# Attention units moved half a unit earlier, and three program blocks joined into one

## The reference

```python
h = rms_norm(x, norm_w[0])
proj = h @ w_in                                    # N_IN = 3668 columns
hm = mlstm_chunkwise(...)                          # 4 heads, running state
score = sum_h w[t,h] * relu(q_idx[t,h] . k_idx[s]) # DSA: indexer
_, sel = lax.top_k(score, 256)                     # each query keeps 256 keys
ha = softmax over the kept keys, times v           # 4 heads
hs = ssd_mixer(...)                                # Mamba-2, 8 heads, running state
x = x + rms_norm(concat([hm, ha, hs]) @ w_out, norm_w[1])
h = rms_norm(x, norm_w[2])
x = x + rms_norm((silu(h @ w_gate) * (h @ w_up)) @ w_down, norm_w[3])
```

## Time and profile before

| | us |
|---|---|
| median of 3 runs | 2692.28 |
| lowest and highest | 2689.32, 2702.49 |
| the profiled execution | 2698.94 |
| its span, first to last instruction | 2697.1 |
| TensorE busy | 2576.8 (96% of the span) |
| mean granted TensorE clock | 0.977 |

### The profile page before, as it was taken

How to read it: one execution, slowest core, us unless ns; L and a number is a source line. 1 busy time by engine, 2 the same in 40 slices (tenths; PEclk the granted TensorE clock), 3 DMA queues, 4 the chain that set the end, 5 groups by cost and what they waited for, 6 DMA issues and landing times. The chain is left out here.

```text
span 2697.1 us, 35783 instructions
## 1 busy us (share of the span) xinstructions
PE 2576.8 (96%) x12676; PEld 2074.7 (77%) x12676; DVE 1832.0 (68%) x3004; ACT 1092.5 (41%) x2078; POOL 1232.3 (46%) x778
## 2 busy tenths in 40 slices
PE   6999998999899999999989999988999999999997
PEld 5678876878688888888766787767877888888886
DVE  5679965773866666666665899648657666666666
ACT  4337435664422232232343463457554223232223
POOL 1348311422754455555433582114227455555545
PEclk8999999899999999999999999989999999999999
DMA  4213321532111111111431233124211111111113
GB/s 136 59 36 94 115 67 35 169 101 77 55 63 47 48 47 52 57 48 61 138 98 36 52 94 112 55 86 148 94 63 63 47 48 47 62 47 62 62 47 133
DMA packets 185793, 199.81 MB, mean 74 GB/s; under 512 B 17680, under 2 KB 161168, under 8 KB 185664
## 3 DMA queue, kind: packets, MB, share of 16 engines
q1 hardware_dynamic: 179904, 177.15, 21.3%
q10 hardware_dynamic: 5760, 20.97, 2.1%
HBM read 157.08 MB, written 38.80 MB: 73 GB/s over the span
## 5 line engine op out<-in xcount | busy, mean ns | idle before, releaser
L2295 POOL TENSOR_TENSOR ring_lo<-ring_sum,ring_hi 128x512 fp32r<-128x512 f32 x200 | 305.4, 1542 | 477.2 <-ACT ring_hi L2383 477.2
L2517 PE MATMUL ps<-form_hi,ring_hi 128*128 128x512 f32 x1232 | 484.5, 393 | 22.6 <-POOL ring_lo L1548 19.7
L2517 PE MATMUL ps<-form_lo,ring_hi 128*128 128x512 f32 x1232 | 482.5, 392 | 0.0
L2517 PE MATMUL ps<-form_hi,ring_lo 128*128 128x512 f32 x1232 | 482.4, 392 | 0.0
L931 PE MATMUL ps<-act_hi,whi 128*128 128x512 f32 x928 | 376.6, 406 | 8.5 <-ACT smr L430 8.4
L2605 DVE TENSOR_TENSOR yacc<-yacc,ps 128x1024 f32<-128x1024 f32 x176 | 214.7, 1220 | 243.7 <-PE ps L2543 243.7
L2383 ACT ACTIVATE ring_hi<-ring_sum 128x512 fp32r<-128x512 f32 x200 | 125.2, 632 | 629.4 <-DVE ring_sum L2593 629.2
L931 PE MATMUL ps<-act_hi,wlo 128*128 128x512 f32 x928 | 366.2, 395 | 0.0
L931 PE MATMUL ps<-act_lo,whi 128*128 128x512 f32 x928 | 365.5, 394 | 0.0
L1350 DVE TENSOR_SCALAR_CACHE_REDUCE ties<-score,kth 128x384 uint8<-128x384 f32 (+5 forms) x396 | 348.4, 942 | 6.1 <-issue 1.7
L636 POOL TENSOR_TENSOR wlo<-raw,whi 128x1024 fp32r<-128x1024 f32 x54 | 131.7, 2439 | 401.2 <-ACT whi L691 401.2
(11 more groups left out here) (333 smaller groups left out, 4606.4 us busy)
## 6 DMA issues: line engine op xcount, KB each, us to landing
raw<-in_w_in SPq DMA_DIRECT2D x56, 512.0 KB, 3.9
ff_raw<-in_w_gate SPq DMA_DIRECT2D x22, 1024.0 KB, 5.4
ff_raw<-in_w_up SPq DMA_DIRECT2D x22, 1024.0 KB, 5.3
ff_raw<-in_w_down SPq DMA_DIRECT2D x22, 1024.0 KB, 4.9
proj_scratch<-stage ACTq DMA_DIRECT2D x40, 512.0 KB, 2.7
wc<-proj_scratch SPq DMA_DIRECT2D x14, 1280.0 KB, 7.1
xmid_scratch<-xres SPq DMA_DIRECT2D x16, 512.0 KB, 2.6
resid<-xmid_scratch SPq DMA_DIRECT2D x16, 512.0 KB, 6.3
```

The lines of the kernel that those rows point to most:

```text
L2295: pool.tensor_tensor(flat_form(ring_lo[slot]), src, flat_form(ring_hi[slot]).bitcast(F32), ALU.subtract)\
L2517: mm = pe.matmul(ps[:, product_bank(r, i), :], w[:, k], a[:, k], start=(k == 0 and m == 0), stop=(k == 3 and m == 2))
```

## The change

1. `U_LATE` is 25 and `LEAD` is 4: call 8 of the attention stands behind eighth 4 of unit 25, and call 35 behind eighth 7 of unit 28. No call is left behind the projection.
2. From step 16 on, ScalarE does a pair's two exponentials together at the odd call, behind the copy of the turned weights.
3. ScalarE loads its table for logarithm and exponential ahead of unit 25, not at the start of stage B.
4. `kept_hi` of blocks 0 to 3 waits for the first half of unit 28 alone, those of 4 to 6 come at the end of stage A, and that of 7 behind the first four `rows` of stage B. The subtractions `kept_lo` of blocks 4 to 7 are all in GpSimd's stage B.
5. All stages are in one block. In place of the meeting, each engine waits for what it takes over: TensorE for the last copy out of PSUM, and further on for the attention's last steps and the cleared places; GpSimd for the last products with `v`; SyncE, ahead of chunk 1, for all eight `kept_lo` (`c_low`).

```diff
-U_LATE = 26
+U_LATE = 25
+LEAD = 4
@@ stage A, ScalarE and TensorE (the same order of calls)
                     if u >= U_LATE:
-                        k = EARLY + 8 * (u - U_LATE)
                         for e in range(8):
+                            k = 8 * (u - U_LATE) + e - LEAD
                             if e == 4:
                                 evac(u, 0)
-                            attend(k + e)
+                            if k >= 0:
+                                attend(EARLY + k)
...
-                for k in range(N_PAIRS, N_PAIRS + 4):
-                    attend(k)
                 rates(NT - 1)
-                kept_hi(NT - 2)
-                kept_hi(NT - 1)
-                for s in range(2):
-                    act.wait_ge(*spilled[s](L, 160))
-                    act.sem_inc(act_fin.sem, 1)
+                for c in range(NT // 2, NT - 1):
+                    kept_hi(act, c)
@@ the new helpers
+            def kept_hi(act, c):
+                act.wait_ge(*projected(N_PROJ - 1, c // (NT // 2)))
+                act.wait_ge(*c_hi(L, c + 1))
+                act.activation(hi_tile(c, 2, 4), kept(c), ACT.Copy).then_inc(c_kept.sem, 1)
+            def kept_lo(pool, c):
+                pool.wait_ge(*c_kept(L, c + 1))
+                pool.tensor_tensor(lo_tile(c, 2, 4), ...).then_inc(c_low.sem, 1)
@@ attend on ScalarE
-                    if k < N_PAIRS:
+                    if k < ONE_PART:
+                        exps(k)
+                    elif k < N_PAIRS and k % 2:
+                        exps(k - 1)
                         exps(k)
@@ b_sync
+                sp.wait_ge(*c_low(L, NT))
                 load_chunk(1)
@@ b_gpsimd
+                pool.wait_ge(*c_pv(L, N_PAIRS // 2))
                 ... the memsets ...
+                for c in range(NT // 2, NT):
+                    kept_lo(pool, c)
@@ b_tensor
-                pe.wait_ge(*b_clear(L, ROWS + 2))
                 pe.wait_ge(*early_in(L, 32))
+                pe.wait_ge(*evicted(N_PROJ - 1, 1))
                 for b in range(3):
                     turns(0, b)
                 load_in(0)
                 turns(0, 3)
+                pe.wait_ge(*c_max(L, N_DOTS))
+                pe.wait_ge(*c_pt(L, N_PAIRS))
                 arguments(0)
                 products(0)
+                pe.wait_ge(*b_clear(L, ROWS + 2))
+                pe.wait_ge(*c_hi(L, NT))
@@ b_scalar
                 for b in range(4):
                     rows(0, b)
+                kept_hi(act, NT - 1)
@@ build
-        together(stages[0][0])
-        for L in range(DEPTH):
-            following = [stages[L + 1][0]] if L + 1 < DEPTH else []
-            together(stages[L][1], stages[L][2], *following)
+        together(*[part for stage in stages for part in stage])
```

More of the change, by code:

```diff
@@ L311, in build @@
         rows_a = sig("rows_a", 5)
-        act_fin = sig("act_fin", 2)
+        c_low = sig("c_low", NT)
         rope_v = sig("rope_v", 3 * 3)
@@ L536, in layer @@
             kept = lambda c: tiles(score[:, sbase[c]:sbase[c] + 2 * P] if c else sinf[:, HALF:HALF + 2 * P])
+            def kept_hi(act, c):
[4 more added lines that the diff above has]
+                pool.wait_ge(*c_kept(L, c + 1))
+                pool.tensor_tensor(lo_tile(c, 2, 4), kept(c), hi_tile(c, 2, 4).bitcast(F32), ALU.subtract).then_inc(c_low.sem, 1)
             x_in = out if L else x
@@ L681, in a_gpsimd @@
                         conv_sum(u - U_XBC)
-                for c in range(NT - 1):
-                    pool.wait_ge(*c_kept(L, c + 1))
-                    pool.tensor_tensor(lo_tile(c, 2, 4), kept(c), hi_tile(c, 2, 4).bitcast(F32),
-                                       ALU.subtract)
+                for c in range(NT // 2):
+                    kept_lo(pool, c)
             def a_scalar(act):
@@ L796, in rates @@
                     act.activation(kept(c), tiles(ps[:, 6 + c % 2, 256:512]), ACT.Copy).then_inc(c_rate.sem, 1)
-                def kept_hi(c):
-                    act.wait_ge(*projected(N_PROJ - 1))
-                    act.wait_ge(*c_hi(L, c + 1))
-                    act.activation(hi_tile(c, 2, 4), kept(c), ACT.Copy).then_inc(c_kept.sem, 1)
                 def gate_columns():
@@ L843, in attend @@
                         rates((k - 8) // AH)
-                    if N_PAIRS <= k < N_PAIRS + KEPT // 2:
-                        kept_hi(2 * (k - N_PAIRS))
-                        kept_hi(2 * (k - N_PAIRS) + 1)
+                    if N_PAIRS <= k < N_PAIRS + NT // 2:
+                        kept_hi(act, k - N_PAIRS)
                 evac(0, 0)
@@ L886, in a_scalar @@
                         attend(2 * (u - U_EARLY) + 1)
+                    if u == U_LATE:
+                        act.preload_act_table_set("natural_log_exp_and_others")
                     if u >= U_LATE:
-                        k = EARLY + 8 * (u - U_LATE)
                         for e in range(8):
+                            k = 8 * (u - U_LATE) + e - LEAD
                             if e == 4:
                                 evac(u, 0)
-                            attend(k + e)
+                            if k >= 0:
+                                attend(EARLY + k)
                         evac(u, 1)
@@ L1116, in a_tensor @@
                     quarter(u, 3)
-                for u in range(U_EARLY + EARLY // 2, U_LATE):
-                    project(u)
+                assert U_EARLY + EARLY // 2 == U_LATE
                 for u in range(U_LATE, N_PROJ):
@@ L1121, in a_tensor @@
                         eighth(u, e)
-                        attend(EARLY + 8 * (u - U_LATE) + e)
-                for k in range(N_PAIRS, N_PAIRS + 4):
-                    attend(k)
+                        k = 8 * (u - U_LATE) + e - LEAD
+                        if k >= 0:
+                            attend(EARLY + k)
             def a_vector(v):
@@ L1405, in a_vector @@
                 rows_out(NT - 1)
-                v.wait_ge(*c_kept(L, NT))
-                v.tensor_tensor(lo_tile(NT - 1, 2, 4), kept(NT - 1), hi_tile(NT - 1, 2, 4).bitcast(F32), ALU.subtract)
             b_clear = sig("b_clear", ROWS + 2)
@@ L1913, in b_scalar @@
             def b_scalar(act):
-                act.preload_act_table_set("natural_log_exp_and_others")
                 def rows(c, b):
```

## The result

| us | before | after |
|---|---|---|
| median of the comparison's runs (7 each) | 2698.38 | 2681.30 |
| lowest and highest | 2689.32, 2702.49 | 2679.20, 2695.29 |
| profiled execution, its span | 2698.94, 2697.1 | 2683.53, 2681.7 |
| mean granted clock | 0.977 | 0.985 |

The ratio is 0.9945, with a 95% interval of 0.9932 to 0.9957: about 15 us faster (the two medians differ by 17.1 us), where 5 were forecast. The time is in the predicted range, 2676 to 2696 us; the gain lies outside the 0.5 to 9 us that had the largest chance. One of the seven executions of the changed kernel took 2695.29 us at a mean granted clock of 0.978. It wasn't profiled, so what it spent them on is open. Note also that the kernel before had a median of 2698 us here, and of 2699 to 2701 over 11 to 23 runs in each of the later comparisons. The 2692.28 on which the forecast was put was a low draw of three.

What follows compares the result with a forecast made beforehand. TensorE, busy in 96% of the span, was taken as the bound, losing time to stalls, the meeting and half clock. Stage A and hand-over gains less half clock gave 0.5 to 6.9 us; 5 was taken: 2687.3 us, range 2676 to 2696.

Steps and rivals of the forecast that it cites:

- The end of stage A: Attention's tail: eighths fill TensorE's waits, gaining 2.5 us, with 1.45 us on top in layer 1.
- the rival of the late attention: Stage A: VectorE isn't ready for unit 25's second half; only about 0 to 2 us gained, 2691 us; chance 0.08.
- Copies first costs and gains nothing: Late attention in stage A: putting copies ahead of exponentials changes nothing, as step 30's turn needs one of each either way.
- The chain to chunk 1: Hand-over: nine links from the last eighth to chunk 1's load, landing at about 474.1 us, half a us later than before.
- The fit of the Trainium skill: Chunk 1's transfer: 2.0 us plus bytes over 436 GB/s, an estimated 5.0 us; the prediction used the trace's 6.6 us.
- The rival that this chain makes the change slower: Hand-over: each us the path to chunk 1 is longer costs 1 us a layer; chance 0.10, 0.04 for over 0.5%.
- one fall per hand-over: TensorE's clock drops to half once in each hand-over, before `arguments` or in the wait for chunk 1.
- a fall lasts 13.7 us: Each half-clock stretch at a hand-over is 13.7 us long; each us shorter adds 0.47 us of gain.
- The case "early": Hand-over: clock falls at about 466.7 us, before `arguments`; gain 2.7 us in layer 0, 4.15 in layer 1.
- the case in which the clock holds: No half clock at either hand-over: gain 5.8 + 7.3 = 13.1 us, 2679.2 us; chance 0.22, including one layer holding.
- What is gained at its start is kept to its end: Stage B: its chunks follow each other by hand-overs between engines, so the gain carries through and nothing is added.
- The sum: Whole kernel: 5 us gained, taken from 0.5 to 7; profiled 2698.94 us becomes 2693.9, carried to the median as 2687.3 us.

Runs made afterwards that it cites:

- the loading in two parts: Changed kernel with chunk 1's load split, the early part issued ahead of SyncE's wait for the last spill: 2688.80 us, ratio 0.9958 to the kernel before.
- the kernel with ten matmuls: Changed kernel with chunk 1 loaded earlier and ten matmuls of unused result in TensorE's waits ahead of `arguments`: 2682.94 us, 0.9937; again 2678.53 us, 0.9930.
- the earlier load by itself: Changed kernel with SyncE waiting ahead of chunk 1 for only four subtractions, not all eight: 2679.94 us, ratio 0.9923; again 2680.90 us, 0.9935.
- the busy TensorE by itself: Changed kernel with ten matmuls of unused result in TensorE's waits ahead of `arguments`, chunk 1 as late as in the changed kernel: 2690.99 us, ratio 0.9974.
- with them in both places: Changed kernel with chunk 1 loaded earlier, ten unused matmuls ahead of `arguments` and ten in each `catr` wait of steps 2 and 3: 2676.40 us, 0.9916.

## Why the prediction was right and where it was not

**The end of stage A: right.** 2.5 us a layer and 1.45 more in layer 1 were forecast, 2.9 and 4.3 came. The four eighths' lead is there in full: from the turn of block 0's result to that of block 1's it is 24.00 us where it was 29.44, 5.44 us less, with 5.45 forecast. VectorE followed, so the rival of the late attention didn't come. The wait for the exponential of step 30 was put at 0.75 us and is 0.62. That layer 1's clock wouldn't fall inside the tail any more was right: both layers take 109.19 us. "Copies first costs and gains nothing" is near (0.2 us a layer).

**The chain to chunk 1: right.** From the turn of the last result, I had 4.4 us to the arguments, 5.5 to the issue of chunk 1 and 12.1 to its turns. The rows of layer 0 have 4.60 (463.90 less 459.30), 5.59 and 12.12 us. Over the four layers profiled the turns came at 12.12 to 13.43 us, each time within 0.1 us of the transfer's landing; layer 1's last spill, 3.3 us where I had 2.6, is the size that was off. The transfer took 6.5 to 7.0 us.

The fit of the Trainium skill ("DMA: Bandwidth & Descriptors", "Anatomy of one DMA"), which is for another issue path, gave an estimate of 5.0 us, and the measurement decides against it here.

The rival that this chain makes the change slower didn't come; that it was a real danger is shown by the loading in two parts, which cost 3.0 us a layer through the last spill and the last part of chunk 0.

**The clock: one fall per hand-over, right; "a fall lasts 13.7 us", wrong.** This is the step that failed, and the mis-sized term of the sum. The falls last 3.4, 6.8, 6.8 and 6.8 us in two profiles of the changed kernel. The case "early" had the second arguments at 483.0 us, 21.0 us behind the turn of the last result; measured were 19.26 (478.56 less 459.30) and 18.00 us in the two executions' layer 0, nearer to the 17.9 us of the case in which the clock holds (479.85). With stretches of their true length the hand-over gains 2.2 us a layer where the forecast of 5 us in all had it lose 0.7. The stretch of 3.4 us that the earlier trace rows held was given little weight. The prediction also had the standing before the fall too long: in the earlier trace rows the clock is at 0.50 from 466.9 us, 2.0 us behind TensorE's last matmul and still within the wait of 3.0. Why the hand-over's falls are shorter after the change is not shown; they begin at other points of it (2.5 to 5.1 us behind the turn of the last result before, 4.4 to 12.5 after).

**"What is gained at its start is kept to its end": wrong by omission.** Stage B was taken to be left alone. But the earlier trace rows showed a second stretch of 13.7 us in it, and I read it only as a duration. The last sentence of the prediction names such stretches as a way to be wrong, but no price for them is in the sum. It comes and goes: over 28 layers of all 14 profiles stage B took 73.4 to 73.7 us with a stretch of 3.4 us in step 2 (16 layers), 74.1 to 74.2 with none (4), 76.6 to 76.7 with one of 13.7 (6) and 78.0 with one of 17.1 (2). The kernel before had the long one in three layers of four, the changed one in none of four: 5.2 us by the means. That the stretch hangs on the wait of 2.33 us for `catr` is shown by filling that wait. What goes with its length is where it begins. Counted from the arguments of chunk 1, that wait ends at 20.05 us in every layer where it isn't filled. All 16 stretches of 3.4 us begin at 20.1 to 21.5 us, all six of 13.7 us at 21.65 to 21.85, and the two of 17.1 us at 19.8 to 19.9, before the wait has ended. What sets the beginning is not shown, so the 5.2 us are measured but their link to the edit rests on four layers of each kernel and on the mean clocks. It isn't the wait's length (2.34 us in both profiles), nor the hand-over's own stretch alone: two layers of the kernel with ten matmuls had none there and 13.7 us in step 2, two others none there and 3.4.

**The sum.** 5 us against 15, made up of 7.2 (forecast 6.4) in stage A, 4.5 (forecast -1.4) in the hand-over and 5.2 (forecast 0) in stage B, 16.9 in all in the profiles. The absolute forecast, 2687.3 us, missed 2681.30 by only 6 us through luck: a baseline 6 us too low made up for half of a gain that was 12 us too small by the medians. By the ratio's own value the change is over 0.5% faster, to which the prediction gave 0.25; the interval, 0.43% to 0.68%, takes in both sides.

## What to carry to other kernels

When a hand-over has both a late transfer and a clock that has fallen, neither pays alone: the earlier load by itself moved the turns of chunk 1 by nothing (12.85 us against 12.12), the busy TensorE by itself by nothing (12.39), both together to 9.9 us, all in layer 0 (and the early load alone moved them to 9.07 us once, when the clock happened to hold). Price a fall of the clock by several stretches of the trace, not by the one next to the edit, and list the falls in all that follows, since a shift of some microseconds can lengthen or shorten them. A wait on TensorE costs more than its length if the clock falls behind it for long, so a few matmuls without use in a known wait can pay (3.8 us a hand-over here, though the totals, 0.9916 with them in both places against 0.9935 with the early chunk 1 alone, have overlapping intervals). Where a small transfer is on the path, an early bulk load belongs behind it: ahead of it, it cost 3.0 us a layer here.

## What the hardware showed beyond what I expected

- The same program (early chunk 1, layer 0) with the same waits (1.00, 0.75 and 0.57 us) kept 2.4 GHz in one execution and fell for 10.2 us in the other. The changed kernel fell for 6.8 us behind waits of 1.00, 0.72 and 0.57 us. The outcome of one execution says little, and six of the kernels here have no second profile.
- A stretch of 3.4 us at 1.2 GHz in step 2 made stage B 0.7 us shorter than none (73.4 against 74.1 us), since the next wait for `catr`, 2.33 us where there was no stretch, is 0.38 us behind one. A stretch's cost hangs on what TensorE would wait for next.
- A load of 128 KB went from 2.2 to 4.3 us in layer 0 and from 2.3 to 5.7 in layer 1 when a load of 1152 KB was issued ahead of it. A spill of 512 KB, issued 0.16 us before that load, went from 2.6 to 3.8 us in layer 0; in layer 1 it took 3.3 to 3.8 us with and without it.
